# One order of products in first units and down units, P1 copied into P2's bank, and ScalarE's copies of sums ahead of its splits of mixed token sums

## The reference

```python
for layer in range(DEPTH):          # DEPTH = 2
    x = x + 0.5 * swiglu_ffn(rms_norm(x, ffn1_norm[layer]), ffn1_w_gate_up[layer], ffn1_w_down[layer])
    h = rms_norm(x, mix_norm[layer])
    y = swa_sink_attention(h, ...) if layer == 0 else mla_attention(h, ...)
    x = x + y
    x = x + 0.5 * swiglu_ffn(rms_norm(x, ffn2_norm[layer]), ffn2_w_gate_up[layer], ffn2_w_down[layer])
return rms_norm(x, final_norm)

def swiglu_ffn(x, w_gate_up, w_down):   # D_MODEL = 1024, D_FF = 2816
    g, u = jnp.split(x @ w_gate_up, 2, axis=-1)
    return (jax.nn.silu(g) * u) @ w_down
```

## Time and profile before

| what | us |
|---|---|
| median of 3 runs (1793.18 to 1796.22) | 1793.22 |
| the profiled execution | 1791.97 |
| its span, first to last instruction | 1790.1 |
| PE busy in the span | 1731.2 |
| DVE busy | 1412.4 |
| ACT busy | 1010.7 |
| POOL busy | 435.4 |
| mean granted TensorE clock | 0.988 |

### The profile page before, as it was taken

One profiled execution on the slowest core, in us unless ns is written; L12 is line 12 of the kernel. 1 busy time (PEld: TensorE's weight loads), 2 busy tenths in 40 slices (PEclk: granted clock), 3 DMA queues, 4 the chain that ended last, 5 costly groups with the idle time before them and its releaser, 6 DMA issues. The chain is left out here.

```text
span 1790.1 us, 35303 instructions
## 1 busy us (share of the span) xinstructions
PE 1731.2 (97%) x12929; PEld 1619.6 (90%) x12929; DVE 1412.4 (79%) x2769; ACT 1010.7 (56%) x2008; POOL 435.4 (24%) x495
## 2 busy tenths in 40 slices
PE   7999999999999999999899999999999999999997
PEld 7999999977889999998899999987867899999986
DVE  6887887667778878867788788766897778788788
ACT  6565665447656556555565565544566566565552
POOL 2333333011023333330233333300000033333310
PEclk8999999999999999999999999999999999999999
DMA  6899999433458998994689999835112489998961
GB/s 191 196 203 207 198 201 225 117 111 89 135 112 187 200 218 198 202 218 129 127 193 208 207 204 205 201 93 127 27 41 60 124 180 200 213 208 195 213 143 58
DMA packets 170377, 293.80 MB, mean 164 GB/s; under 512 B 22689, under 2 KB 56670, under 8 KB 170206
## 3 DMA queue, kind: packets, MB, share of 16 engines
q0 software_dynamic: 66816, 121.66, 39.8%
q1 hardware_dynamic: 101824, 168.13, 30.8%
q10 hardware_dynamic: 1566, 1.74, 0.3%
HBM read 163.29 MB, written 2.10 MB: 92 GB/s over the span
## 5 line engine op out<-in xcount | busy, mean ns | idle before, releaser
L1994 PE MATMUL bank<-h_all,w_all 128*128 128x256 f32 x2352 | 676.0, 287 | 26.8 <-DVE w_all L1316 15.2
L1995 PE MATMUL bank<-h_all,w_all 128*128 128x256 f32 x2352 | 669.8, 285 | 0.0
L1996 PE MATMUL bank<-h_all,w_all 128*128 128x256 f32 x2352 | 669.5, 285 | 0.0
L823 POOL DMA_DIRECT2D work<-r_all x348 | 306.8, 1033 | 980.3 <-DVE w_all L1316 613.1
L1994 PEld LDWEIGHTS bank<-h_all,w_all 128*128 128x128 f32 x2352 | 455.6, 194 | 37.2 <-DVE w_all L1316 25.9
L1995 PEld LDWEIGHTS bank<-h_all,w_all 128*128 128x128 f32 x2352 | 456.0, 194 | 0.0
L1996 PEld LDWEIGHTS bank<-h_all,w_all 128*128 128x128 f32 x2352 | 455.8, 194 | 0.0
L1316 DVE TENSOR_TENSOR w_all<-work,w_all 128x512 fp32r<-128x512 f32 x352 | 233.7, 687 | 100.3 <-ACT w_all L941 99.4
L1316 DVE TENSOR_TENSOR w_all<-r_all,w_all 128x512 fp32r<-128x512 f32 (+1 forms) x356 | 299.8, 863 | 2.2 <-ACT w_all L941 0.4
L941 ACT ACTIVATE w_all<-r_all 128x512 fp32r<-128x512 f32 (+1 forms) x356 | 267.6, 769 | 56.5 <-PE bank L1996 55.1
L1994 PE MATMUL bank<-y_all,w_all 128*128 128x256 f32 x896 | 254.8, 284 | 10.1 <-DVE w_all L1316 10.1
(11 more groups left out here) (226 smaller groups left out, 2669.1 us busy)
## 6 DMA issues: line engine op xcount, KB each, us to landing
work<-r_all POOLq DMA_DIRECT2D x348, 256.0 KB, 4.7
r_all<-ffn_gu SPq DMA_DIRECT2D x88, 512.0 KB, 4.9
r_all<-r_all POOLq DMA_DIRECT2D x116, 256.0 KB, 6.7
r_all<-ffn_gu SPq DMA_DIRECT2D x88, 256.0 KB, 6.1
work<-ffn_gu SPq DMA_DIRECT2D x88, 256.0 KB, 5.2
r_all<-ffn_d SPq DMA_DIRECT2D x32, 512.0 KB, 5.1
x_f<-ffn_e SPq DMA_DIRECT2D x24, 384.0 KB, 5.4
work<-ffn_d SPq DMA_DIRECT2D x32, 256.0 KB, 4.2
```

The lines of the kernel that those rows point to most:

```text
L823: pool.dma_start(chain[g % CHAIN], plain[(u + 2) % 3][:, part * S:(part + 1) * S], accum_op=ALU.add).then_inc(chain_sum[g % CHAIN], 16)
L1994: t.matmul(o, wh, xh, start=c == 0 and not on, stop=False, skip_group_check=on)
L1995: t.matmul(o, wh, xl, start=False, stop=False, skip_group_check=on)
L1996: last = t.matmul(o, wl, xh, start=False, stop=c == PAIRED - 1, skip_group_check=on)
```

## The change

- TensorE takes P1(u), P4(u-1), P2(u), and then P6(u), P3(u-1), P5(u), P7(u). In the first down unit after gate units ("opening", u10 and u22) P3(u-1) comes ahead of P6(u). Semaphore counts follow (`product_order`).
- ScalarE copies P1 into `D_BANK` in every unit, and P2's matmuls add to it there. P2 waits for that copy (`e_1`). In u1 one further matmul into `D_BANK` runs with P1, with its start flag. `s_1` is gone, and so is VectorE's add of line 1600 and, in down units, its first of two additions into `xT`. `first_normed` multiplies the bank by `r_x`.
- On ScalarE the copy of P1 is ahead of the splits of FU(u+1) and `single_copy`. The copy to `u_3` is ahead of `high_mixed`; VectorE's `low_mixed` moves behind its split of FB in the next unit. In u1 the silu of unit 0 and of u1 move behind the split of FC and the copy to `u_2`.
- In u1 of FFN 0 the spread of the RMS factor on TensorE moves behind P6, and VectorE's sums and splits for it move ahead of the RMS values. On VectorE `low_fill(f, FA, 2)` moves ahead of the first gate quarter.
- In `PLAIN_ORDER` two entries change places. P1(u2) waits for `z_gate` instead of the whole of unit 0.
- Four of the 16 transposes at the end move from u28 and u29 to behind the FFN.

```diff
@@ product_order
-        out += [(1, u), (2, u), (4, u - 1), (6, u), (3, u - 1), (5, u), (7, u)]
+        late = [(3, u - 1), (6, u)] if opening(u) else [(6, u), (3, u - 1)]
+        out += [(1, u), (4, u - 1), (2, u)] + late + [(5, u), (7, u)]
@@ 
-PLAIN_ORDER = [(0, False), (1, False), (2, False), (0, True), (3, False), (1, True), (2, True), (3, True)]
+PLAIN_ORDER = [(0, False), (1, False), (2, False), (0, True), (1, True), (3, False), (2, True), (3, True)]
@@ scalar, ffn
                     if u > 1:
                         high_fill(f, FB, u)
-                        high_fill(f, FU, u + 1)
-                        single_copy(f, u + 2)
-                    if gate:
-                        act.wait_ge(prod_done, product_count(f, 1, u))
+                    act.wait_ge(prod_done, product_count(f, 1, u))
+                    if at > 0:
                         act.wait_ge(e_2, at)
-                        a.activation(s_1, b[:, 0:HN], ACT.Copy).then_inc(e_1, 1)
-                    if u == 1:
-                        high_fill(f, FU, 2)
-                        single_copy(f, 3)
+                    a.activation(D_BANK[:, 0:HN], b[:, 0:HN], ACT.Copy).then_inc(e_1, 1)
+                    high_fill(f, FU, u + 1)
+                    single_copy(f, u + 2)
...
-                    if u == 1:
-                        act.wait_ge(z_gate, f + 1)
-                        a.activation(z_0, z_0, ACT.Silu).then_inc(z_silu, 1)
-                    if gate:
+                    if gate and u > 1:
                         silu(f, u, 0)
                     high_fill(f, FC, u)
...
                         a.activation(u_2[u % 2], b[:, 0:HN], ACT.Copy).then_inc(e_6, 1)
+                    if u == 1:
+                        act.wait_ge(z_gate, f + 1)
+                        a.activation(z_0, z_0, ACT.Silu).then_inc(z_silu, 1)
+                        silu(f, u, 0)
...
-                    if q is not None:
-                        high_mixed(y_mix, combine_count(f, q, True), q % PAIRED)
                     if gate:
                         act.wait_ge(prod_done, product_count(f, 7, u))
                         act.wait_ge(e_5, at)
                         a.activation(u_3, b[:, 0:HN], ACT.Copy).then_inc(e_7, 1)
+                    if q is not None:
+                        high_mixed(y_mix, combine_count(f, q, True), q % PAIRED)
@@ vector
+            def first_normed(f, u, m):
+                at = order_of(f, u)
+                dve.wait_ge(misc_free, m + 2)
+                dve.wait_ge(prod_done, product_count(f, 2, u))
+                if u > 2:
+                    dve.wait_ge(e_4, at - 1)
+                elif f > 0:
+                    dve.wait_ge(e_4, order_of(f, 1))
+                v.tensor_tensor(g_0[u % 2], D_BANK[:, 0:HN], r_x[:, 0:HN], ALU.mult).then_inc(e_2, 1)
...
-                        v.tensor_tensor(g_0[u % 2], D_BANK[:, 0:HN], s_1, ALU.add).then_inc(e_2, 1)
...
-                    if f == FFNS - 1 and u > DOWN_END[1]:
+                    if f == FFNS - 1 and DOWN_END[1] < u < NU - 2:
@@ tensor, product
-                    elif q == 2 and at > 0:
-                        pe.wait_ge(e_2, at)
+                    elif q == 2:
+                        pe.wait_ge(e_1, at + 1)
...
-                    on = q in (3, 4, 6, 7)
+                    on = q in (2, 3, 4, 6, 7)
+                    if q == 1 and u == 1 and c == 0:
+                        t.matmul(D_BANK[:, 0:HN], wh, xh, start=True, stop=True)
@@ tensor, ffn
-                product(f, 5, 1, (0, 2))
+                product(f, 5, 1)
+                product(f, 6, 1)
                 if f == 0:
                     spread(m + 1)
-                product(f, 5, 1, (2, PAIRED))
-                for q in (6, 7):
-                    product(f, q, 1)
+                product(f, 7, 1)
```

More of the change, by code:

```diff
@@ L108, in fill_count, with opening @@
     return (6 * NU - 3) * f + at + 1
+def opening(u):
+    return UNITS[u][0] == "D" and UNITS[u - 1][0] == "G"
 def product_order():
@@ L1065, in silu @@
                 buf = g_1 if half else g_0[u % 2]
-                act.wait_ge(gr_done, half_count(f, u, half))
+                if half:
+                    act.wait_ge(gr_done, (TILES - 1) * f + UNITS[u][1])
+                else:
+                    act.wait_ge(e_2, order_of(f, u) + 1)
                 a.activation(buf, buf, ACT.Silu).then_inc(silu_done, 1)
@@ L1459, in first_sums @@
                     mixed(1)
+                    pair_mix(f, 3)
+                    mixed(2)
+                    mixed(3)
+                    low_fill(f, FB, 1)
                 if f == 0:
@@ L1585, in ffn @@
                         low_fill(f, FB, u)
-                    opening = not gate and UNITS[u - 1][0] == "G"
-                    if opening:
-                        dve.wait_ge(prod_done, product_count(f, 1, u))
-                        x_added(UNITS[u][2], 0, b).then_inc(e_1, 1)
+                    q = COMBINED.get(u - 1)
+                    if q is not None:
+                        low_mixed(y_mix, combine_count(f, q, True), q % PAIRED)
                     low_fill(f, FU, u + 1)
@@ L1611, in ffn @@
                         first_gate(f, m)
+                        low_fill(f, FA, 2)
                     if gate:
-                        normed_gate(f, u, 0, m)
-                    if not gate:
+                        first_normed(f, u, m)
+                    else:
+                        c0 = UNITS[u][2]
                         dve.wait_ge(prod_done, product_count(f, 2, u))
-                        dve.wait_ge(e_1, at + 1)
                         x_added(c0, 0, D_BANK[:, 0:HN]).then_inc(e_2, 1)
```

50 lines of the change are left out of this document (19 added, 31 removed).

## The result

| | us |
|---|---|
| the kernel after, median of 6 runs (1810.31 to 1812.91) | 1811.66 |
| the kernel before beside it, median of 6 runs (1793.18 to 1796.22) | 1794.3 |
| ratio, 95% interval | 1.0094 [1.0082, 1.0106] |
| forecast | 1799.8 (1791.5 to 1806) |

A forecast was written before the change was run, and what follows sets the result against it. TensorE, holding 97% of the span, was taken to bound the kernel by issue time plus stalls. Pairs +11.2, starts -5.0 and end +0.4 gave +6.6: 1798.6 in the profiled execution, 1799.8 as median, range 1791.5 to 1806.

The forecast's parts named there:

- pairs: Pairs of gate units with mixing: changed TensorE stalls at P4, P2, P6 and P7 cost +11.2 us over four FFNs.
- starts: Starts of the four FFNs: P2(u1) waits for P1's copy, but P7(u1) no longer for unit 0's silu; -5.0 us.
- end: End of the kernel: four transposes move back, VectorE's work stays the same, its last transpose ends later; +0.4 us.
- Everything behind keeps its time: VectorE in the pairs: the removed add only makes room for a wait of about 0.5; later operations keep their times.
- P6's stall before: P6(u6) in the kernel before: a marked stall of 0.32, put behind ScalarE's P1 copy of line 1083.
- The copy into PSUM: ScalarE's copy of P1 into P2's bank: taken as 0.36, like the copy into SBUF; P2 stalls 0.28 with restart.
- the term for FFN 2: Start of FFN 2: P2 begins 1.9 later, yet P6(u2) comes at 887.6 against 889.2; -1.6 us.
- FFN 0: Start of FFN 0: TensorE stands 5.7 before P2, then runs partly at 1.2 GHz; +0.8 us, between -2 and +4.
- rival (c): Starts of FFN 0, 2 and 3: the clock stays at 1.2 GHz after P2's wait; +11, 1804, chance 0.12.
- a fall of the clock in FFN 1 to 3: Sign at the starts of FFN 1 to 3: if the granted clock falls there, the forecast is wrong.
- (a): Rival in the pairs: only P4's stall comes, P2's does not; +1.0, 1794.2, chance 0.18.
- (b): Rival in the mixing units: VectorE's saved add reaches the copy of line 1124; -13.9, 1779.3, chance 0.10.

The follow-up runs named there:

- Experiment 1: The kernel after with VectorE's weight split for the next unit's P1 and P2 behind both first-half operations of the late unit (1809.11) or between them (1798.75).
- e8: The kernel after with VectorE's split of the mixed sums back at the end of the mixing unit instead of in the next unit; 1809.56.
- e6: The kernel before with only ScalarE's copy of P1 moved ahead of its FU(u+1) weight split and the summed weights' copy; 1795.66.
- e14: The kernel after with e9's and e10's edits, plus ScalarE's P1 copy ahead of its P6 weight split in units behind mixing units; 1794.26.
- e1: The kernel after with VectorE's weight split for the next P1 and P2 behind both operations of the late unit's first half; 1809.11.
- e9: The kernel after with VectorE's weight split for the next P1 and P2 between the two operations of the late unit's first half; 1798.75.
- e12: The kernel after with P2 again right behind P1 and P4 third, P1's sums still copied into P2's bank; 1861.39 in one run.
- e2: The kernel before with only the start's silus of u0 and u1 moved later on ScalarE and P1(u2) waiting for unit 0's sums; 1788.54.
- e10: The kernel after with product 5 of unit 1 ahead of product 2; 1804.39.
- e11: The kernel before with e2's moved silus and the change's tail, four transposes of units 28 and 29 behind the last weight splits; 1787.94.
- e15: e14 with VectorE's multiplication leading to the last product's copy ahead of its split of unmixed tiles, in mixing units that a gate unit follows; 1779.08.
- e16: e2 with VectorE's multiplication leading to the last product's copy ahead of its split of unmixed tiles, where a gate unit follows; 1775.29.
- e5: The kernel before with only ScalarE's copy of the last product moved ahead of the mixed sums' split in the mixing units; 1799.48.
- e7: The kernel before with the change's product order, opening units and ScalarE order, but P1 copied to SBUF and added by VectorE; 1863.29.

## Why the prediction was wrong

The direction and most of the mechanism were right; the size was not. In the two profiles the terms stand so:

| term | forecast | traces |
|---|---|---|
| pairs | +11.2 | +17.3 |
| starts (with what FFN 3 gives back in u3 and u4) | -5.0 | -1.1 |
| P4(u29) of FFN 0 to 2 | none | +1.1 |
| end | +0.4 | +0.7 |
| sum | +6.6 | +18.0 |

The profiles lie 21.0 apart, 3.0 more than the sum: 0.9 ahead of the first FFN and 2.1 between FFN 0 and 1, where the clock fell once in the kernel after and not before, in code that the change doesn't touch. The medians lie 17.4 apart: the profiled execution of the kernel before is 2.3 under its median, that of the kernel after 1.2 above.

**The pairs: the step "Everything behind keeps its time" failed.** It took the saved add as turned into a wait and left VectorE "back to back" to the multiplication that leads to the copy. That multiplication came at 10.76 and not at 10.52. 0.07 is P2's bank, ready at 4.58 and not at 4.51; the other 0.17 is the FA split, whose ScalarE half waits for P2 to be through. This wait was there to be found: the forecast moved P2 back by one product, and asked who reads P2's bank, but not who overwrites its weights. Experiment 1 shows that the place of that split alone moves the stall from 1.11 to 0.75. So per pair: P4 1.11 instead of 0.90, P2 0.30 instead of 0.28. Settled pairs cost 1.40 - 0.80 = 0.60 (forecast 0.37), first pairs 1.40 - 0.51 = 0.89 (0.67), the last ones 0.37 (0.17), where P7 of the opening unit loses 1.10; e8 shows 0.19 of that to be VectorE's mixed split. Per FFN 2 x 0.89 + 3 x 0.60 + 2 x 0.37 = 4.3, in four 17.3. In FFN 3 the first pair carries more, told below. P4(u29), which the forecast left out, loses 1.31 instead of 0.94 in FFN 0 to 2.

**P6's stall before was read wrongly, without harm to the sum.** The forecast put it behind the copy of line 1083. The bracket in the earlier trace rows names VectorE's weight split, and e6 shows it to be that. In the change P6 loses nothing because P4 and P2 have lost 1.3 ahead of it: in e8, where VectorE's mixed split stands ahead of FB again, FB starts at 604.05 and ends at 604.74, and P6(u8) has its turn at 604.98, after FB all the same. That the forecast of no stall at P6 came true says nothing for its reason.

**The copy into PSUM: right.** Rows gave 0.36, the trace has 0.36 to 0.37, and P2's stall is 0.30. The Trainium skill, ScalarE: Activation LUTs (the tip that ScE to PSUM is the faster way), isn't borne out for these 256 columns: into PSUM the copy takes 0.36 to 0.37, into SBUF 0.36 to 0.39. e14 shows that this stall is ScalarE's queue and not the copy, and that taking it away gives nothing.

**The starts: the term for FFN 2 and the missing one for FFN 3 failed.** From P1(u1) to P1(u3) the kernel after takes 3.2 less in FFN 1 (forecast 3.0 less), 1.5 less in FFN 3 (1.2), 0.05 more in FFN 2 (1.6 less), 1.9 more in FFN 0 (0.8). P7(u1) of FFN 1 came 7.59 after P1(u1) (forecast 7.8), P4(u1) lost 1.10 (0.9), at full clock, as said. In FFN 2 P2 began where it was forecast, but the clock then fell; TensorE's P2(u1) and the window behind it, kernel after:

```profile
887.22 0.35 PE L2000 MATMUL bank<-h_all,w_all 128*128 128x256 f32 x1 [1.89 <-DVE w_all L1323]
```
```profile
887.70:891.20 3.50, 3.50 (x19) 3.50 (x19) 1.35 (x3) 2.58 (x4) 2.45 (x4) 0.51 0.86 149
```

and the same in e1, whose start is the same code with the same wait of 1.89:

```profile
886.60:890.10 3.50, 3.50 (x32) 3.50 (x31) 2.46 (x4) 2.70 (x4) 2.38 (x3) 1.00 0.87 149
```

19 matmuls against 32. e1 took 1.5 less to P1(u3), about the forecast gain. e8, e9 and e12 have the same start and the same wait of 1.89 to 1.90 too: behind it the clock fell in e8 and e9 and stayed full in e12. So rival (c) came true in part, with a fall that three of five profiles show. The forecast had named a fall of the clock in FFN 1 to 3 as a sign that it is wrong. The range took it in, but not on top of a term for the pairs that was 6.1 too small; and (c) was added up too low: 11.2 + 4 - 3.0 + 0.4 is 12.6, 1805.8, not +11 and 1804.

In FFN 3 the miss is a stall of 1.36 at P4(u2) and one of 1.36 instead of 1.11 at P4(u3). ScalarE's timeline of the kernel after:

```profile
1474.09 0.63 ACT L947 ACTIVATE w_all<-work 128x512 fp32r<-128x512 f32 x1 [2.16 <-DMA work<-r_all]
1474.62 0.36 ACT L1129 ACTIVATE work<-bank 128x256 f32<-128x256 f32 x1
```

The copy stands behind split FD, which waits for a transfer. Before, the transfer was no cause of a stall: P4 had its turn 1.44 later, and u2 itself came later. All kernels here with the moved silus show such stalls in FFN 3 (e2 loses 0.68 at P4(u2), 1.64 at P6(u3) and 1.2 at P4(u3), and gives all of its gain back): in the first units of FFN 3 the loads set the pace. How much is given back differs: e10 starts another 1.4 quicker than the kernel after, yet loses 1.1 less in u3 and u4 together. That was in no term. That the load of the gains, issued between two weight loads there, is what delays them was not tried.

**FFN 0: right in kind.** TensorE issued nothing of the units from 34.0 to 40.13, 6.1 (forecast 5.7); the granted clock was 0.50 in the window from 40.1 to 44.6 behind it.

**The end: right.** The transposes end at 1787.79, 23.3 ahead of the end of the span, as before (1766.77 and 1790.1); e11 shows the whole tail to be worth nothing.

**The rivals.** (a) is excluded by P2's stall of 0.26 to 0.30 in every pair. (b) needed the multiplication by `r_x` to start before P2's bank is readable; it starts with it, at 4.58. (c) came true in FFN 2 alone. None of them named an operation that waits for P2 on account of its weights.

## What to carry to other kernels

When a product is moved back in TensorE's order, list for its bank and for its operands' buffers everyone who waits for it to be through: the writer that refills the weights is moved back as well. Before an order is changed on the engine that shows the wait, follow the late operand to its head; here two exchanges on VectorE (e9, and the one of e15 and e16) gave 13 and 13 to 15 us, while exchanges on ScalarE carried a stall to another product (e5, e14) or did nothing (e6). Where two things that a product waits for end within 0.1 of each other, as the copy and FB at P6, move one of them and look (e6) before building on either. A wait on a full queue should be filled with the independent operation that also parts two dependent ones.

## What the runs showed of the hardware

- Two VectorE operations of 128x256 start 0.33 to 0.34 apart when independent, 0.45 to 0.53 when the second waits for the first's result by a semaphore; for one of 128x512 ahead of such a reader it is 0.71 against 0.60. In the kernel after it is 0.45 from line 1541 to the up quarter's product and from 1556 to 1535, where that wait is the first or only one of the second operation, and 0.52 from 1541 to 1547, where another wait stands ahead of it. The 1556 to 1535 pair takes 0.52 in e16 (1540 to 1519), whose code has another wait ahead of it. That this is the reason was not tested by itself.
- ScalarE copies 128x256 from bank to bank in 0.36 to 0.37, as from bank to SBUF.
- The granted clock after a stall isn't fixed by the stall: behind 1.89 at the same place it fell in three profiles (kernel after, e8, e9) and stayed at 1.00 in two (e1, e12); behind eight stalls of 2.96 it fell four times, and the same sum in two pieces (0.92 and 2.04) kept it full in seven of eight places; behind e7's 28 stalls of 2.01 it fell 17 times, behind the kernel after's 28 of 1.11 never.
- The table load ahead of unit 0's silu took 1.28 again (535.09 in FFN 1 of the kernel after), and the silu began at 536.38, right behind it. The Trainium skill, ScalarE: Activation LUTs (Table-load gate), gives about 2.7 with the drain; no drain shows here, so 1.28 is the whole price.
